# A decoder layer in split fp32: three products of a projection into one set of 256 PSUM columns

## The reference, cut to what matters

```python
h = x @ w_in                                   # 2048 -> 15360
q, k, v, z_attn, u_pool, z_pool, g_pre = split(h)
# 3 dilations x 8 heads of causal window attention, mixed by their softmax denominators
y_attn = mix(o_1, o_2, o_3) * silu(z_attn)
# trailing mean over 2, 4, 8, 16 tokens minus the token, a 256x256 map per group, a scale
y_pool = pool_mixer(u_pool, w_pool) * pool_scale * silu(z_pool)
g_attn, g_pool = split(sigmoid(g_pre + b_gate))
merged = g_attn * (y_attn @ w_proj_attn) + g_pool * (y_pool @ w_proj_pool)
out = layer_norm(2 ** 0.25 * x + merged @ w_out, gamma, beta)
```

## Time and profile before

| | before |
|---|---|
| time, median of 3 runs (lowest to highest) | 961.31 us (961.26 to 961.7) |
| span of the profiled execution, first to last instruction | 959.4 us |
| PE busy | 948.2 us, 5355 matmuls and 5355 weight loads |
| DVE busy | 633.2 us |
| ACT busy | 422.8 us |
| from HBM | 174.87 MB |

### The profile page before, as it was taken

The page is one execution under the profiler, slowest core; times in us unless marked ns, Lnnn a source line. Parts: engine busy times, 40 slices in busy tenths (PEclk is TensorE's granted clock), DMA queues, the critical chain, the costliest instruction groups (busy, mean ns, idle before and its releaser), DMA issues.

```text
span 959.4 us, 15088 instructions
## 1 busy us (share of the span) xinstructions
PE 948.2 (99%) x5355; PEld 839.9 (88%) x5355; DVE 633.2 (66%) x989; ACT 422.8 (44%) x585; POOL 0.2 (0%) x4
## 2 busy tenths in 40 slices
PE   8999999999999999999999999999999999999996
PEld 6998898898898898898898899888888888888884
DVE  6767667667667667667567568665666666665666
ACT  5444344344354354354354354545445444543330
POOL 0000000000000000000000000000000000000000
PEclk9999999999999999999999999999999999999998
DMA  9644544445544444444544445655555555555532
GB/s 354 248 170 180 175 175 174 176 173 177 175 175 175 175 175 175 175 175 175 175 175 175 175 175 214 225 176 204 190 176 194 186 187 178 208 207 195 182 126 87
DMA packets 26387, 177.18 MB, mean 185 GB/s; under 512 B 3327, under 2 KB 3583, under 8 KB 5759
## 3 DMA queue, kind: packets, MB, share of 16 engines
q1 hardware_dynamic: 26064, 173.79, 50.3%
q10 hardware_dynamic: 308, 3.19, 0.9%
HBM read 174.87 MB, written 2.10 MB: 184 GB/s over the span
## 4 chain that ended last, share of the span: by engine, by line
PE 97%; DVE 1%; DMA 1%; SPq 0%; ACT 0%; issue 0%; DVEq 0%
PE proj_ps L328 40%; PE proj_ps L330 20%; PE attn_ps L328 6%; PE attn_ps L311 4%; PE attn_ps L313 4%; PE attn_ps L312 4%; PE attn_ps L330 3%; PE value_ps L312 3%; PE value_ps L313 3%; PE value_ps L311 3%; PE mixed_ps L416 1%; DMA xt_raw<-in_xt 1%; PE mixed_ps L311 1%; PE mixed_ps L313 1%; PE mixed_ps L312 1%; PE attn_ps L377 1%
## 5 line engine op out<-in xcount | busy, mean ns | idle before, releaser
L328 PE MATMUL proj_ps<-xt,w_hi 128*128 128x512 f32 x1664 | 585.3, 396 | 1.9 <-DVE xt L703 1.0
L330 PE MATMUL proj_ps<-xt,w_lo 128*128 128x256 f32 x1664 | 466.5, 280 | 0.0
L681 DVE TENSOR_TENSOR w_lo<-w_raw,w_hi 128x1024 fp32r<-128x1024 f32 x322 | 379.0, 1220 | 81.3 <-ACT w_hi L537 79.9
L328 PEld LDWEIGHTS proj_ps<-xt,w_hi 128*128 128x128 f32 x1664 | 312.1, 188 | 75.5 <-DVE w_lo L681 1.3
L537 ACT ACTIVATE w_hi<-w_raw 128x1024 fp32r<-128x1024 f32 x322 | 322.4, 1051 | 53.9 <-PE mixed_ps L313 27.1
L330 PEld LDWEIGHTS proj_ps<-xt,w_lo 128*128 128x128 f32 x1664 | 314.3, 189 | 0.0
L556 ACT ACTIVATE corr<-proj_ps 128x256 f32<-128x256 f32 x104 | 40.0, 385 | 290.8 <-PE proj_ps L330 290.8
L695 DVE TENSOR_TENSOR qk_f<-proj_ps,corr 128x256 f32<-128x256 f32 x48 | 20.3, 424 | 80.9 <-ACT corr L556 80.9
L328 PE MATMUL attn_ps<-yp,w_hi 128*128 128x512 f32 x128 | 45.9, 397 | 0.0
L328 PE MATMUL attn_ps<-ya,w_hi 128*128 128x512 f32 x128 | 45.6, 395 | 0.0
L311 PE MATMUL attn_ps<-w_hi,xt 128*128 128x384 f32 x128 | 42.9, 335 | 0.0
(11 more groups left out here) (149 smaller groups left out, 878.6 us busy)
## 6 DMA issues: line engine op xcount, KB each, us to landing
w_raw<-in_weights SPq DMA_DIRECT2D x159, 1024.0 KB, 4.8
xt_raw<-in_xt SPq DMA_DIRECT2D x4, 512.0 KB, 7.4
w_raw<-in_weights SPq DMA_DIRECT2D x4, 512.0 KB, 8.6
res<-in_x_rows ACTq DMA_DIRECT2D x1, 2048.0 KB
out_rows<-res SPq DMA_DIRECT2D x8, 256.0 KB, 2.1
gamma<-in_gamma_row ACTq DMA_DIRECT2D x1, 1024.0 KB
mask<-in_mask SPq DMA_DIRECT2D x1, 576.0 KB, 11.1
ident<-in_identity SPq DMA_DIRECT2D x1, 64.0 KB, 11.6
```

The costliest lines, as they stand in the source:

```text
L328: mm(bank, w_hi[:, slot, cols], tile.rearrange("p a s -> p (a s)"), start=first, stop=False)
L330: done = mm(bank[:, SEQ:2 * SEQ], w_lo[:, slot, cols], tile[:, 0, :], start=False, stop=last)
L681: tt(w_lo[:, slot, cols], w_raw[:, slot, cols], w_hi[:, slot, cols].bitcast(F32), ALU.subtract).then_inc(lo_split, 1)
```

## The change

- In `chunk` the 512- and the 256-column matmul of each k become three of 256 columns, by `product`, all into columns 0 to 255 of the bank. In `mix` likewise: for one tile of keys three of 256 columns, for the other three of 128.
- Nothing is left to be summed: `correction`, `halves_summed`, `corr`, `corr_pair`, `mixed_corr` and `qk_f` go. ACT writes the high part of q and k from PSUM, and DVE subtracts it from PSUM, which frees the bank. ACT copies u from PSUM (`u_copied`), and takes the tanh of z and the gates from PSUM.
- DVE no longer forms the sigmoids as half of one plus tanh. It multiplies (tanh + 1) by the PSUM columns, and the factor one half moves to a later operation (`mix`, `half_scale`, the split of `merged`).
- PE's waits change with it: `next_bank` counts 8 freed banks a step and waits for `u_copied`; in stage B it waits for the tanh of the tile before (`tanh_done`) and for `pair_free`.

```diff
@@ -325,18 +316,18 @@
                             between(k)
                         bank, tile, first, last = moving(k)
                         cols = slice(k * P, (k + 1) * P)
-                        mm(bank, w_hi[:, slot, cols], tile.rearrange("p a s -> p (a s)"),
-                           start=first, stop=False)
-                        done = mm(bank[:, SEQ:2 * SEQ], w_lo[:, slot, cols], tile[:, 0, :],
-                                  start=False, stop=last)
+                        done = product(bank, w_hi[:, slot, cols], w_lo[:, slot, cols],
+                                       tile[:, 0, :], tile[:, 1, :], first, last)
                 done.then_inc(chunk_done, 1)
 
-            def next_bank(n, j, i):
-
-                pe.wait_ge(proj_free, FROM + banked(n, j) + i * banked_per(n))
+            def next_bank(j, i):
+
+                pe.wait_ge(proj_free, FROM + banked(j) + i * A_BANKED)
+                if j == Z_POOL:
+                    pe.wait_ge(u_copied, i + 1)
 
             def from_x(bank):
-                return lambda k: (proj_ps[:, bank, :], xt[:, k, :, :], k == 0, k == KT - 1)
+                return lambda k: (proj_ps[:, bank, 0:SEQ], xt[:, k, :, :], k == 0, k == KT - 1)
 
             def x_arrives(k):
...
@@ -407,16 +398,14 @@
                 pe.wait_ge(v_split, FROM + i * TT + TT)
                 pe.wait_ge(mixed_free, FROM + i)
 
-                out = mixed_ps[:, :].rearrange("p (a q) -> p a q", a=2)
                 for g in range(GROUPS):
                     v = slice(g * P, (g + 1) * P)
                     for kt in range(TT):
 
                         queries, cols = ((slice(0, SEQ), slice(0, SEQ)), (slice(P, SEQ), slice(SEQ, PTW)))[kt]
-                        mm(out[:, :, queries], v_hi[:, kt, v], pt[:, g, :, cols],
-                           start=(g == 0 and kt == 0), stop=False)
-                        done = mm(out[:, 1, queries], v_lo[:, kt, v], pt[:, g, 0, cols],
-                                  start=False, stop=(g == GROUPS - 1 and kt == TT - 1))
+                        done = product(mixed_ps[:, queries], v_hi[:, kt, v], v_lo[:, kt, v],
+                                       pt[:, g, 0, cols], pt[:, g, 1, cols],
+                                       g == 0 and kt == 0, g == GROUPS - 1 and kt == TT - 1)
                 done.then_inc(mixed_ready, 1)
...
 
             def from_y(k):
 
                 bank, kk = k // HALF, k % HALF
-                return (attn_ps[:, bank * 512:(bank + 1) * 512], (ya, yp)[bank][:, kk, :, :],
+                return (proj_pair[:, bank, :], (ya, yp)[bank][:, kk, :, :],
                         kk == 0, kk == HALF - 1)
 
             with pe.Fori(0, B_STEPS) as i:
                 for j in range(B_CHUNKS):
-                    bank = (B_FIRST + j) % 2
-                    if j % 3 < 2:
-                        chunk(B_FIRST, j, i, B_CHUNKS, from_x(bank))
+                    d, z = j // 3, j % 3
+                    if z < 2:
+
+                        pe.wait_ge(tanh_done, 2 * A_STEPS + 2 * (d - 1) + z + 1 + i * (2 * B_STEPS))
+                        chunk(B_FIRST, j, i, B_CHUNKS, from_x(z))
                     else:
 
                         pe.wait_ge(y_split, HEADS)
                         pe.wait_ge(yp_split, POOL_TILES // 2)
+                        pe.wait_ge(pair_free, FROM + d + i * B_STEPS)
                         chunk(B_FIRST, j, i, B_CHUNKS, from_y)
-                    next_bank(B_FIRST, j, i)
 
             def out_products(n, kk, t):
...
@@ -544,18 +535,9 @@
                 for half in range(2):
                     hi_part((n + j) % RING, half)
 
-            def correction(n, j, i, per, pair=False):
+            def projected(n, j, i, per):
 
                 act.wait_ge(chunk_done, FROM + n + j + 1 + i * per)
-                if pair:
-
-                    act.wait_ge(proj_free, FROM + banked(n, j) - 2 + i * banked_per(n))
-                    activation(corr_pair[:, :, :], proj_pair[:, :, SEQ:2 * SEQ], ACT.Copy).then_inc(act_evac, 1)
-                else:
-                    b = (n + j) % 2
-                    activation(corr[:, b, :], proj_ps[:, b, SEQ:2 * SEQ], ACT.Copy).then_inc(act_evac, 1)
-
-                act.wait_ge(proj_free, FROM + banked(n, j) + i * banked_per(n))
 
...
-
-                        act.wait_ge(proj_free, FROM + banked(0, j) + i * A_BANKED)
-                    if not V_FIRST <= j < V_FIRST + GROUPS:
-                        correction(0, j, i, A_CHUNKS)
+                    if j < V_FIRST:
+                        projected(0, j, i, A_CHUNKS)
+                        activation((q_hi[:, j // 2, :], keys[:, j // 2, 0, :])[j % 2],
+                                   proj_ps[:, j % 2, 0:SEQ], ACT.Copy).then_inc(act_evac, 1)
                     if j in (Z_ATTN, Z_POOL):
-
-                        act.wait_ge(proj_free, FROM + banked(0, j) + 1 + i * A_BANKED)
-                        z = int(j == Z_POOL)
-                        activation(th_gate[:, z, :], gate_f[:, z, :], ACT.Tanh, scale=0.5).then_inc(tanh_done, 1)
-
-
-                act.wait_ge(mixed_ready, i + 1)
-                activation(mixed_corr[:, :], mixed_ps[:, SEQ:2 * SEQ], ACT.Copy).then_inc(mixed_corr_done, 1)
+                        projected(0, j, i, A_CHUNKS)
+                        activation(th_gate[:, int(j == Z_POOL), :], proj_ps[:, j % 2, 0:SEQ], ACT.Tanh,
+                                   scale=0.5).then_inc(tanh_done, 1)
+                    if j == U_POOL:
+                        projected(0, j, i, A_CHUNKS)
+                        activation(u_pad[:, PAD:PAD + SEQ], proj_ps[:, j % 2, 0:SEQ],
+                                   ACT.Copy).then_inc(u_copied, 1)
 
 
...
-                    correction(B_FIRST, j, i, B_CHUNKS, pair=j % 3 == 2)
                     if j % 3 < 2:
-
-                        act.wait_ge(proj_free, FROM + banked(B_FIRST, j) + 1 + i * B_CHUNKS)
-                        activation(th_gate[:, j % 3, :], gate_f[:, j % 3, :], ACT.Tanh,
+                        projected(B_FIRST, j, i, B_CHUNKS)
+
+                        act.wait_ge(pair_free, FROM + j // 3 + i * B_STEPS)
+                        activation(th_gate[:, j % 3, :], proj_ps[:, j % 3, 0:SEQ], ACT.Tanh,
                                    bias=half_bias[:, bass.ds(i * 4 + ((j % 3) * OT + j // 3), 1)],
                                    scale=0.5).then_inc(tanh_done, 1)
...
-                dve.wait_ge(act_evac, banked(n, j) + 1 + i * banked_per(n))
-                tt(dst, proj_ps[:, (n + j) % 2, 0:SEQ], corr[:, (n + j) % 2, :], ALU.add).then_inc(proj_free, 1)
-
-            def freed(n, j, i):
-                dve.wait_ge(proj_free, FROM + banked(n, j) + 1 + i * banked_per(n))
+            def freed(j, i):
+                dve.wait_ge(proj_free, FROM + banked(j) + 1 + i * A_BANKED)
+
+            def silu_doubled(dst, z, j, i):
+
+                dve.wait_ge(tanh_done, z + 1 + i * 2)
+                stt(out=dst, in0=th_gate[:, z, :], scalar=1.0, in1=proj_ps[:, j % 2, 0:SEQ],
+                    op0=ALU.add, op1=ALU.mult).then_inc(proj_free, 1)
 
             nc.vector.memset(zeros[:, :].bitcast(F32), 0.0).then_inc(zeros_ready, 1)
...
                     split_lo(0, j + AHEAD, i, A_CHUNKS)
                     if j < V_FIRST:
                         g = j // 2
                         hi, lo = ((q_hi[:, g, :], q_lo[:, g, :]), (keys[:, g, 0, :], keys[:, g, 1, :]))[j % 2]
-                        halves_summed(qk_f[:, j % 2, :], 0, j, i)
-                        freed(0, j, i)
-                        chain.link(copy(hi, qk_f[:, j % 2, :]))
-                        tt(lo, qk_f[:, j % 2, :], hi.bitcast(F32),
-                           ALU.subtract).then_inc(qk_split, 1)
+
+                        dve.wait_ge(act_evac, j + 1 + i * (2 * GROUPS))
+                        tt(lo, proj_ps[:, j % 2, 0:SEQ], hi.bitcast(F32), ALU.subtract).then_inc(proj_free, 1)
                     if j == SCORES_AFTER:
                         masked_max(i)
                     if j == Z_ATTN:
-                        halves_summed(gate_f[:, 0, :], 0, j, i)
-                        sigmoid(0, 1, i, 2)
-                        chain.add(tt(silu_za[:, :], gate_f[:, 0, :], gate[:, 0, :], ALU.mult))
+                        silu_doubled(silu_za[:, :], 0, j, i)
                     if j == V_FIRST + GROUPS - 1:
                         for t in range(TT):
 
                             dve.wait_ge(v_hi_done, i * TT + t + 1)
                             tt(v_lo[:, t, :], v_ps[t][:, :], v_hi[:, t, :].bitcast(F32),
                                ALU.subtract).then_inc(v_split, 1)
-                    if j == U_POOL:
-                        halves_summed(u_pad[:, PAD:PAD + SEQ], 0, j, i)
                     if j == Z_POOL:
-                        halves_summed(gate_f[:, 1, :], 0, j, i)
-                        sigmoid(1, 2, i, 2)
-
-                        chain.add(stt(out=tile_of(szp, i), in0=gate_f[:, 1, :],
```

(59 more changed lines are left out.)

44 lines of the change are left out of this document (19 added, 25 removed).

## The result

The changed kernel takes 979.42 us (979.12 to 979.58, 4 runs) beside 961.28 (961.04 to 961.70, 4 runs) of the kernel before: the ratio is 1.0186, 95% interval 1.0174 to 1.0199. The forecast was 970.3, the range 959 to 980. The direction was right and the time lies just inside the range, but the loss, 18.1 us, is twice the 9.0 of the sum.

A forecast was written before the change was run, and what follows sets the result against it. PE was taken as the bound, its slots times their length. Stage A chunks +2.0, stage B chunks +4.1 and `mix` +2.9 us gave +9.0 on 961.3, so 970.3 us; range 959 to 980.

The forecast's parts named there:

- the 9.0 of the sum: Whole kernel: stage A chunks +2.0 us, stage B chunks +4.1 and `mix` +2.9, everything else nothing.
- The bound, and what lies off it: PE's slots set the time; lighter ACT and DVE work gains nothing, and no new PE waits cost anything.
- `mix`: Four matmuls a group become six, 128-column slots at about 115 ns: +0.12 us for each of 24 groups, +2.9 us.
- What three 256-column matmuls cost: Chunk products: 118.1 ns a slot, 354.3 a product, read from 47 pool map slots; +2.0 us stage A, +4.1 stage B.
- The scores' 118.8: Alternative slot price from 8 slots of the scores, 356.3 ns a product: +12.9 us in all, 974 us.
- The pair's price: A 512- plus a 256-column matmul now costs 352.6 ns on the mean in stage A, 348.9 in stage B.
- The tie: A load lasts about as long as 256 columns stream; 512-column slots hide it, 256-column slots pay a small excess.
- The first: Rival: 256-column slots in long runs settle to the quick pairs' pace, at no extra cost; 957 us, chance 0.10.
- The second: Rival: product and pair cost the same, only `mix` pays; 964.2 us, chance 0.11 including what lies up to the forecast.
- the third: Rival: instruction supply bounds PE, 96 loads and matmuls a chunk for 64; at 62 ns each 1004 us, chance 0.07.
- The fourth: Rival, chance 0.07: chunk slots run over 120 ns with nothing waited for; products at slow pairs' 0.36 us give 981.

The follow-up runs named there:

- experiment 6: 32 unused bytes a partition added behind `row_kind`, shifting the tiles behind: kernel before 958.13 us (0.9966), changed kernel 979.75 us (1.0189).
- Experiments 3 and 4: Changed kernel, low-order products only: weight loads of 64 or 32 columns, 961.17 and 966.43 us; 240 or 192 columns streamed, 946.46 and 943.88 us.
- after_pad32: Changed kernel with 32 more unused bytes a partition, so later tiles lie 32 past a multiple of 64 again: 979.75 us, 1.0189.
- experiments 6 and 7: Kernel before: later tiles shifted 32 bytes, 958.13 us; that plus smaller `mix` matmuls, 965.19; only stage A's tiles and `merged` shifted, 955.23. Changed kernel shifted: 979.75.
- experiment 2: Kernel before with only the matmuls of `mix` split into smaller ones: 959.77 us, 0.9981.

## Why the prediction came out as it did

- **The bound, and what lies off it: right.** All of the difference is in PE's slots. DVE and ACT lost 108 us of work between them, and it gave nothing; no wait of PE appeared. The count of matmuls was exact.
- **`mix`: right.** +2.6 us for +2.9, with 128-column slots that did not run at half price.
- **The chunks: the step "What three 256-column matmuls cost" took 118.1 ns for a slot, and it is 120.0.** Times three it is 360.0 for 354.3, which is 5.7 ns for each of 1920 products or 10.9 us, more than the whole error of 9.1 us. The slip was to carry a pace over from the pool map, whose tiles lay otherwise in SBUF; experiment 6 moved them by 32 bytes and the pace went to 120. The scores' 118.8 was the better of the two and was named as an end by the rows, 974.
- **The pair's price was read right, and hid how large the step is.** In the kernel before, stage A runs its pairs mostly at 353.3 and not at 346.7 ns; after, the product runs at 360.0 in both stages. Against the quick pace the third matmul costs 13.3 ns, against the slow one 6.7; over all 1920 products, from the table and the chunks of stage A, it cost 18.2 us or 9.5 ns.
- **The tie: partly wrong.** I held that a 512-column slot pays nothing and a 256-column one pays for being as long as its load. In fact 512, 384 and 256 columns take 226.7 (stage C), 173.7 (118.14 to 123.35, 30 slots) and 120.0 ns, that is 213.3, 160.0 and 106.7 at 2.4 GHz and 13.3 to 13.7 more each. So at these three widths, with the tiles as the changed kernel has them, every matmul pays it, and the cost of the change is one more payment for each k. It is no constant: at 240 columns a slot pays 12.0 on the mean, and with `merged` 32 bytes off a 512-column slot pays 20. Experiments 3 and 4 leave the load some part: the payment shrinks with shorter loads, and another limit lies close below. What the 13.3 ns consist of stays open. The Trainium skill, TensorE: Matmul & The Clock Gate, section "Wait — 56ns, not 53.3ns?", has the form that fits these three widths, a fixed price besides the columns, and its 2.5 ns is a fifth of what these split-fp32 matmuls show.
- **Stage C: not foreseen.** Its -2.5 us come from 32 bytes of layout (experiment 6), not from the arithmetic of the change. The same 32 bytes made the chunks on `ya` and `yp` 1.6 us longer, so that the changed kernel without the shift takes nearly the same (after_pad32, 979.75). The time lies 0.6 us inside the range by luck: with 360.0 for a product the prediction's own sum gives 981, outside it, and what brought the time back in, the slots of stage C or else those on `ya` and `yp`, was no term of the sum.
- **The rivals.** The first (settling to the streaming pace, 957) fell: after 2304 equal slots there was no settling. The second (a product as long as a pair) fell with it. Of the third, code is fetched once as before and nothing waits for it. The fourth was the nearest. Its 981 comes from a product of 0.36 us, and the product is 360.0 ns; less the 2.5 us of stage C that is close to the measured time. Its reason holds in half: a slot in a chunk did cost more than in the pool map of the kernel before. But it is not the way of the slow pairs, every slot is 120.0, and with its tiles moved by 32 bytes the pool map costs the same.
- **What stays open.** Why pairs have two paces, and what picks one: addresses move it (experiments 6 and 7), and so does what ran ahead (experiment 2). No run separated the two.

## What to carry to other kernels

Where TensorE is the bound and its columns are given, count matmuls. Each one more with a load of its own cost 13 ns here where 512-column slots ran at their quickest, in a chunk or in the output projection, and 7 ns where they were slow already, while work taken off the other engines was worth nothing. Take the price of a slot from a stretch with the same tiles, since 32 bytes of layout moved the slots of one stage by 6 ns and those of another by 2, which for three slots a product was the error of this forecast. When a small edit shifts the tiles behind it, time the shift by itself before the edit gets the credit.

## What the runs showed of the hardware that was not expected

- Tiles 32 bytes past a multiple of 64, counted from `xt`, against tiles on it: 512-column slots of stage C, where the tile is loaded, 233 and 226.7 ns; 256-column slots of the pool map, where it is streamed, about 118 and 120. Both hold in both kernels.
- A sequence of matmuls of 512 and 256 columns has two steady paces, 346.7 and 353.3 ns a pair, each kept for whole chunks of 5.5 us and more; smaller matmuls in `mix` moved stage A from one to the other and made the kernel 0.2% faster.
- Loads of 64 columns in place of 128 in two of three matmuls, with as narrow an output, took 9.4 ns off the product of 360.0; loads of 32 took 6.1.
